# Hybrid encoder layer on one core: large SBUF buffers at multiples of 2048 bytes, two copies of the masked scores, decays on ScalarE

## The reference

```python
def hgrn2_direction(q, v, f_logit, lb):
    f = lb + (1.0 - lb) * jax.nn.sigmoid(f_logit)
    return gla_chunk_scan(q, 1.0 - f, v, jnp.log(f))
...
    qh = jax.nn.sigmoid(heads(hq))
    vh = jax.nn.silu(heads(hi))
    o_fwd = hgrn2_direction(qh, vh, heads(hf_fwd), lbf)
    o_bwd = flip(hgrn2_direction(flip(qh), flip(vh), flip(heads(hf_bwd)), lbb))
    o = rmsnorm(o_fwd + o_bwd, hg_out_norm) * jax.nn.silu(heads(hg))
```

## Time and profile before

| | us |
|---|---|
| median of 3 runs (lowest, highest) | 1182.69 (1180.28, 1183.96) |
| the profiled execution | 1190.63 |
| its span, first to last instruction | 1188.1 |
| PE busy | 1104.6 |
| DVE busy | 573.1 |
| POOL busy | 446.0 |
| ACT busy | 337.8 |
| mean granted PE clock, share of full | 0.95 |

### The profile page before, as it was taken

The page is one execution under the profiler, slowest core; times in us unless marked ns, Lnnn a source line. Parts: engine busy times, 40 slices in busy tenths (PEclk is TensorE's granted clock), DMA queues, the critical chain, the costliest instruction groups (busy, mean ns, idle before and its releaser), DMA issues.

```text
span 1188.1 us, 13305 instructions
## 1 busy us (share of the span) xinstructions
PE 1104.6 (93%) x4936; PEld 886.6 (75%) x4936; DVE 573.1 (48%) x775; ACT 337.8 (28%) x495; POOL 446.0 (38%) x202
## 2 busy tenths in 40 slices
PE   6999999999998898989898798978999999999996
PEld 5888888888886676868675466757888888888884
DVE  5654455450001749677684544486454554510004
ACT  6322222222222333233226332333222222222211
POOL 1544444444444443122220500645444444434420
PEclk9999999999999899989898689978999999999996
DMA  7333332323332132121120000313333333233201
GB/s 218 107 96 99 89 105 88 99 84 98 98 99 89 60 106 71 37 54 54 36 71 18 18 1 1 108 35 89 88 98 96 88 93 101 79 98 91 89 15 71
DMA packets 174137, 93.10 MB, mean 78 GB/s; under 512 B 11476, under 2 KB 169752, under 8 KB 174104
## 3 DMA queue, kind: packets, MB, share of 16 engines
q1 hardware_dynamic: 173680, 92.55, 26.6%
q10 hardware_dynamic: 424, 0.10, 0.1%
HBM read 90.54 MB, written 2.10 MB: 78 GB/s over the span
## 4 chain that ended last, share of the span: by engine, by line
PE 87%; DVE 10%; ACT 1%; issue 1%; DMA 0%; POOL 0%; DVEq 0%; SPq 0%; ACTq 0%
PE ps L671 24%; PE ps L673 24%; PE ps L672 24%; PE ps L925 2%; PE ps L818 2%; PE ps L781 1%; PE ps L782 1%; PE ps L783 1%; PE ps L855 1%; DVE xT L1056 1%; PE ps L940 1%; DVE TMP L1055 1%; PE ps L888 1%; DVE S L1294 1%; DVE S L1317 1%
## 5 line engine op out<-in xcount | busy, mean ns | idle before, releaser
L353 POOL TENSOR_TENSOR WL<-raw,WH 128x1024 fp32r<-128x1024 f32 x168 | 405.1, 2414 | 673.2 <-ACT WH L415 673.2
L671 PE MATMUL ps<-XH,WH 128*128 128x512 f32 x912 | 369.1, 405 | 17.9 <-DVE XL L1034 8.0
L673 PE MATMUL ps<-XH,WL 128*128 128x512 f32 x912 | 364.8, 400 | 0.0
L672 PE MATMUL ps<-XL,WH 128*128 128x512 f32 x912 | 364.3, 399 | 0.0
L415 ACT ACTIVATE WH<-raw 128x1024 fp32r<-128x1024 f32 (+1 forms) x170 | 176.1, 1038 | 564.6 <-PE ps L673 545.6
L671 PEld LDWEIGHTS ps<-XH,WH 128*128 128x128 f32 x912 | 175.3, 192 | 60.2 <-DVE XL L1034 10.1
L673 PEld LDWEIGHTS ps<-XH,WL 128*128 128x128 f32 x912 | 175.0, 192 | 38.9
L672 PEld LDWEIGHTS ps<-XL,WH 128*128 128x128 f32 x912 | 175.2, 192 | 38.5
L673 PE MATMUL ps<-hh,WL 128*128 128x512 f32 x352 | 139.3, 396 | 0.0
L672 PE MATMUL ps<-hl,WH 128*128 128x512 f32 x352 | 138.9, 395 | 0.0
L671 PE MATMUL ps<-hh,WH 128*128 128x512 f32 x352 | 138.2, 393 | 0.0
(11 more groups left out here) (158 smaller groups left out, 972.8 us busy)
## 6 DMA issues: line engine op xcount, KB each, us to landing
raw<-ffn_w_gate SPq DMA_DIRECT2D x44, 512.0 KB, 3.8
raw<-ffn_w_up SPq DMA_DIRECT2D x44, 512.0 KB, 3.8
raw<-ffn_w_down SPq DMA_DIRECT2D x32, 448.0 KB, 3.3
raw<-w_in SPq DMA_DIRECT2D x22, 512.0 KB, 3.8
raw<-ffn_w_down SPq DMA_DIRECT2D x16, 512.0 KB, 3.6
raw<-w_out SPq DMA_DIRECT2D x8, 512.0 KB, 3.6
xin<-x SPq DMA_DIRECT2D x4, 512.0 KB, 6.5
raw<-w_in SPq DMA_DIRECT2D x8, 256.0 KB, 3.4
```

The source lines that it names most:

```text
L353: pool.tensor_tensor(WL[:, s, 0:size], raw[:, s, 0:size], WH[:, s, 0:size].bitcast(fp32), ALU.subtract).then_inc(lo_done, 3 if n == 2 else 1)
L671: nc.tensor.matmul(dst, WH[:, s, w], xh, start=first, stop=False)
L672: nc.tensor.matmul(dst, WH[:, s, w], xl, start=False, stop=False)
L673: return nc.tensor.matmul(dst, WL[:, s, w], xh, start=False, stop=last)
```

## The change

Three things change. The small tensors are placed first, with a pad of 208 float32 (`row_pad`) behind them, so that all the large buffers start at a multiple of 2048 bytes, and every row of 512 float32 with them. `SD` gets two copies, one for even and one for odd heads, and in SCHEDULE a unit's half comes ahead of `values(h - 1)` instead of behind it. The decays and the keys 1 - f are made by ACT in `head_sigmoid`, in two instructions behind each sigmoid of a decay; DVE's `gates` keeps only the three products.

```diff
@@ mixer_schedule
             out.append(("score", h, g))
+            if g < 9:
+                fill()
             if not g and h:
                 out.append(("values", h - 1))
-            if g < 9:
-                fill()
@@ buffers: xT, raw, WH, WL are taken from here ...
-        xT = sb("xT", [P, KD, TOK])
-        raw = sb("raw", [P, NSLOT, SLOT])
-        WH, WL = sb("WH", [P, NSLOT, SLOT], f32r), sb("WL", [P, NSLOT, SLOT], f32r)
@@ ... and put behind the small ones
         rt_root, rt = sb("rt_root", [P, 6, TT]), sb("rt", [P, 6, TT])
+
+        sb("row_pad", [P, 208])
+        xT = sb("xT", [P, KD, TOK])
+        raw = sb("raw", [P, NSLOT, SLOT])
+        WH, WL = sb("WH", [P, NSLOT, SLOT], f32r), sb("WL", [P, NSLOT, SLOT], f32r)
         RSB = sb("RSB", [P, TOK])
@@
-            ("Qh", [P, 2, TOK], fp32), ("KS", [P, 2, TOK], fp32), ("SD", [P, TOK], fp32),
+            ("Qh", [P, 2, TOK], fp32), ("KS", [P, 2, TOK], fp32), ("SD", [P, 2, TOK], fp32),
@@ head_sigmoid (ACT)
                                      ACT.Sigmoid).then_inc(proj_sig, 1)
+                if t:
+                    f, at = Fg[:, h % 2, t - 1, :], 4 * (t - 1) + h
+                    act.wait_ge(proj_sig, 3 * h + t + 1)
+                    nc.scalar.activation(f, f, ACT.Identity, bias=lb[:, at:at + 1], scale=lb1[:, at:at + 1]).then_inc(decay_done, 1)
+                    act.wait_ge(decay_done, 4 * h + 2 * t - 1)
+                    if h >= 2:
+                        act.wait_ge(pv_done, h - 1)
+                    nc.scalar.activation(W[:, h % 2, (K_F, K_B)[t - 1], :], f, ACT.Identity, bias=ones[:, :], scale=-1.0)\
+                        .then_inc(decay_done, 1)
@@ gates (DVE)
                 dve.wait_ge(proj_sig, 3 * h + 3)
-                for d in range(2):
-                    at = 4 * d + h
-                    step(nc.vector.tensor_scalar(Fg[:, b, d, :], Fg[:, b, d, :], lb1[:, at:at + 1], lb[:, at:at + 1], ALU.mult, ALU.add))
-
-
+                dve.wait_ge(decay_done, 4 * h + 4)
                 if h >= 2:
                     dve.wait_ge(pv_done, h - 1)
-                nc.vector.tensor_scalar(W[:, b, K_F, :], Fg[:, b, 0, :], -1.0, 1.0, ALU.mult, ALU.add)
-                step(nc.vector.tensor_scalar(W[:, b, K_B, :], Fg[:, b, 1, :], -1.0, 1.0, ALU.mult, ALU.add))
@@ diagonal (DVE); take_level and values use SD[:, h % 2] likewise
-                if h:
-                    dve.wait_ge(pv_done, h)
-                nc.vector.tensor_tensor(SD[:, :].rearrange("p (c t) -> p c t", c=TT),
+                if h >= 2:
+                    dve.wait_ge(pv_done, h - 1)
+                nc.vector.tensor_tensor(SD[:, h % 2, :].rearrange("p (c t) -> p c t", c=TT),
```

More of the change, by code:

```diff
@@ L224, in encoder_layer @@
         keys_grown, keys_mixed = sem("keys_grown"), sem("keys_mixed")
+        decay_done = sem("decay_done")
         scores_ready, scores_masked, scores_copied = sem("scores_ready"), sem("scores_masked"), sem("scores_copied")
@@ L848, in values @@
                         if c == t:
-                            s = SD[:, t * P:(t + 1) * P]
+                            s = SD[:, h % 2, t * P:(t + 1) * P]
                         elif c == t ^ 1:
@@ L1237, in take_level @@
                 dve.wait_ge(scores_masked, 8 * h + 1 + lv)
-                nc.vector.copy_predicated(SD[:, :].rearrange("p (b s j) -> p s b j", s=2, j=half), masks[:, lv, :],
+                nc.vector.copy_predicated(SD[:, h % 2, :].rearrange("p (b s j) -> p s b j", s=2, j=half), masks[:, lv, :],
                                           ps[4 + (11 * h + 1 + lv) % 2][:, :]).then_inc(scores_masked, 1)
```

## The result

Measured side by side, the changed kernel takes 1174.68 us (median, 1173.43 to 1176.71) and the kernel before 1182.53 (1180.28 to 1183.96): ratio 0.9937, 95% interval 0.9914 to 0.9960. That is 7.9 us faster. I had forecast no change, 1.8 us slower than before: the wide range (1168 to 1191.5) held, the forecast's own (1181 to 1187.5) did not, and the direction was wrong.

The account below looks back on a forecast made before the run. PE, busy 1104.6 of 1188.1 us, was taken as the bound. Terms +3.4 (forward decay), -1.6 (copies), 0 and 0 summed to +1.8 us: 1184.5 median, forecast range 1181 to 1187.5, wide range 1168 to 1191.5.

Parts of the forecast that it names:

- The placement: Big products and loads: aligning buffers to 2048 bytes counted 0, bounds -50 to +7.0 us for the products.
- (a): Big products of the FFNs: 229 and 233 ns at the same addresses, so the address alone doesn't set the pace.
- (c): Head values: V rows inside or crossing a 2048-byte line both take 3.57 us for 32, so crossing costs nothing there.
- (b): Big products take 13 to 17 ns more than 256-column products at 216 ns; placement could remove this excess.
- The forward decay: Forward units, heads 1 to 3: ACT's two new instructions delay the mixed keys, PE stands 1.15 us each, +3.4 us.
- The backward decay: Backward units: DVE starts 2.4 us earlier but meets POOL's split one step later; gain 0.2 us, counted as nothing.
- The copies: Two SD copies and earlier half remove PE waits of 0.72 us (head 1) and 0.92 us (head 3): -1.6 us.
- The loads: PE waits on a load only at the start, 5.85 us of `xin`; counted 0, page estimate 0.5 us off.
- A: Rival, chance 0.20: placement quickens the big products; 1134 us at the full 13 ns, 1174 if a fifth goes.
- B: Rival, chance 0.16: POOL's split misses DVE's chain at the backward unit; long waits 2.9 us, time 1176 to 1170.
- C: Rival, chance 0.12: the slower product pace comes in both FFNs; +7.0 us, 1191.5.
- D: Rival, chance 0.14: slack behind the forward unit goes through ACT's queue, a second PE wait opens; +4.5 us, 1189.

Follow-up runs that it names:

- everything at 1024: Kernel before with only placement changed: everything big 1024 bytes past a multiple of 2048; 1176.37 us, ratio 0.9941.
- late split: ACT's split moved behind the copy of the mixed keys: in the kernel of placement and copies 1168.90 us, in the changed kernel 1167.11 us.
- late and held split: Late split without decays on ACT, the split also held behind the first work after head 2's backward sigmoid; 1166.11 us, ratio 0.9827.

## Why the prediction was wrong, point by point

- **The placement (counted 0): wrong, and the step that failed.** I had three pieces of evidence and took the wrong one. The term that I put at nothing is worth some -8 us by the pace of the products. (a) Two paces at one address made me say that the address does not set the pace. The distance of two addresses does, up to one case: at 64 bytes 228.9 ns is what three other profiles show in both FFNs, and the profiled execution of the kernel before showed 233.3 in its second FFN besides. It was this case that I looked at. (c), which I took as nearest in kind, asked whether a row that crosses a 2048-byte line is slower. It isn't, as the kernel with everything at 1024 shows; but a crossing was the wrong question. The right one was how the two operands of a product stand to each other. (b), the excess over the 216 ns of the 256-column products, contained the gain, but 2.2 of the 13 ns. With 3168 x 2.2 = 7.0 us in the FFNs the term is -7.0, and some 1 us more for the 192 wide products, whose mean spacing fell from some 233 ns by 5 to 7. The big products between the levels of the tree, with other products among them, hardly gained (229.9 to 229.8 ns).
- **The forward decay (+3.4): right, a little too large.** Three waits of 0.96 to 0.99 us instead of 1.15, on KM, behind the forward units of heads 1, 2 and 3: +2.9. Decay and key took 0.82 and 0.72 us, estimated 0.83 and 0.72.
- **The backward decay (0): right in all its steps, 0.2 us a head short.** Counted from the sigmoid's start, DVE was to start at 2.29 and did at 2.34; ACT's split at 2.15, measured 2.14; POOL's at 3.29, measured 3.26; one of DVE's two-input products was to stand 2.2 us, and `KS` did for 2.1. The runs with the late split showed that it is this collision that makes 2.0 us of the wait, and also what I hadn't said: most of the 2.4 us that the decays on ACT seemed to offer was the collision of L1174, and only 0.15 to 0.2 was the move itself. The Trainium skill, SBUF — State Buffer, Who interferes with whom, says that a VectorE instruction with two SBUF inputs contends with a GpSimd instruction that reads SBUF; the trace agrees (2.83 us for `KS` against 0.68 without a meeting). The section says that a TENSOR_SCALAR, which has a single tensor input, can contend too, in a mode that uses both ports; no run shows the mode, but the key's TENSOR_SCALAR (L1176 of the late-split kernel) takes 2.48 us in the meeting and 0.43 without.
- **The copies (-1.6): right in place, perhaps too small.** The waits of 0.72 and 0.92 us are gone; the run alone gave -3.8 with -2.2 as the nearest end of the interval, of which 0.7 was in the attention, where I hadn't looked.
- **The loads (0): nothing else is shown.** The first load of `xin` took 5.85 us before and 5.56 in the changed kernel. But over all profiles with `xin` at a multiple of 256 bytes that have it on the chain it took 5.49 to 6.00 us, and over those without, 5.55 to 6.19. The 0.5 us that I estimated from the page are not to be told from this spread.
- **The sum.** With the measured terms: -7.0 - 1.0 for the pace, +2.9 for the forward waits, -0.5 for the long waits (5.18, 5.11 and 5.18 to 5.01, 4.93 and 5.00), -1.6 for the copies: -7.2 against -7.9 measured. The agreement is closer than the measurement can bear out (-10.2 to -4.7), and the sum leaves out the attention, where one wait grew by 1.4 us and one shrank by 0.7.
- **The rivals.** A (0.20) is what came, near its weak end of "a fifth of it goes, 1174": 2.2 of 13 ns went. It named neither the second operand nor the distance. B did not come in the changed kernel; brought about by the late and held split it gave nearly what it promised, 3.1 us waits (2.9 forecast) and a clock that stays up behind two of seven of them. C had the right suspicion, a pace that can change, in the wrong direction. D did not open: there is one wait behind each forward unit.
- **The rule that putting the arithmetic on ACT costs** (the Trainium skill, ScalarE: Activation LUTs, Rules for kernel authors) agrees with the decays alone, +3.6 us; but these came from ACT's queue behind the forward unit, not from two slower instructions on the path.

## What to carry to other kernels

Where PE streams back to back and loads new weights for each product (here 512 columns of float32r, the type of `WH`, `WL`, `XH` and `XL`), put the weights and the streamed operand at addresses whose distance is a multiple of 256 bytes; alignment of either to anything else did nothing here, and aligning one alone made it 1% slower. Look for the pace in the spacing of outputs, not in the durations of instructions. When an instruction is taken off an engine that collides with another, ask first where the other will land: here moving a split by one place in a queue took 2 us off a long wait, and moving four instructions to another engine 0.2.

## What the runs showed of the hardware that I had not expected

- **The load of weights and the stream of a product are not independent.** Five distances (modulo 256 bytes) gave 226.7 to 233.3 ns for a product of 512 float32r columns. The Trainium skill, TensorE: Matmul & The Clock Gate, Step-by-step: what each phase is for, says that PE has two independent SBUF read ports and that loading the next weights takes no read bandwidth from the running matmul. By that rule all rows of the table would be the same; the measurement decides, and at most distances it costs 1 to 3%. Its cause inside the memory stays open.
- **Legal is not quick.** The same skill, SBUF — State Buffer, Operand start alignment, allows any start at a multiple of the element's size and says that nothing was timed. The run at a distance of 32 bytes (1196 us) and those of placement alone at 0 (1167 to 1176) show what it can be worth: some 2%.
- **The pattern of the granted clock differs between executions of one kernel.** The kernel before has executions at 0.956 with 1178 to 1181.5 us and others at 0.95 with up to 1191. A part worth 2 to 4 us is better read from PE's idle time and pace in a trace than from a median of six.
